# Transposing X unscaled and bringing the norm's factor in as a row, in a two-block fp32 kernel on one Trainium2 core

## The chip, the cores and the metric

The kernel runs on one core of a Trainium2 chip. The metric is the device time of one execution in microseconds (us). TensorE is called PE below, its weight loads PEld, VectorE is DVE, ScalarE is ACT, GpSimd is POOL and SyncE is SP, as in the profile.

## The reference

X is 256 rows of 1024 numbers (fp32). Two blocks of a transformer run over it: first one mixer and its MLP, then a second block of two layers (a convolution and an attention, each with an MLP). Cut to what matters here:

```python
def rms_norm(x, g):
    return x * lax.rsqrt(jnp.mean(x * x, axis=-1, keepdims=True) + EPS) * g
# first block
h = rms_norm(x, g_mix_pre)
x = x + rms_norm(mixer(h) @ w_out, g_mix_post)
h = rms_norm(x, g_ff_pre)
x = x + rms_norm(jnp.square(jax.nn.relu(h @ w_ff_in)) @ w_ff_out, g_ff_post)
# second block, for each of two layers; sh, sc, g are modulation vectors of length 1024
h = rms_norm(x, mix_norm_g) * (1.0 + sc1) + sh1
x = x + g1 * (conv if layer == 0 else attention)(h)
h = rms_norm(x, mlp_norm_g) * (1.0 + sc2) + sh2
x = x + g2 * (jnp.square(jax.nn.relu(h @ w1)) @ w2)
```

So there are six norms of X. They are called norm 0 to norm 5 below: ahead of the mixer's input product (0), the first MLP (1), the convolution (2), the second MLP (3), the attention's QKV product (4) and the third MLP (5).

## The kernel before

**Products.** Every weight is streamed once from HBM in units of 128 x 2048 numbers (1 MB), through a ring of four slots. ACT writes a rounded copy `hi` of a unit (L345), DVE the remainder `lo` (L356), and PE takes three products for each pair of tiles: hi by hi, hi by lo, lo by hi (L407). The activation is split in the same way, into `hTh` and `hTl`, and it is needed transposed: 8 pieces (k = 0 to 7) of 128 channels by 256 rows of X. `unit_w` multiplies one unit of weights by 4 or 8 of the pieces and runs k in its innermost loop, `unit_x` the same with the activation as the stationary side. One unit of an MLP's first product is 48 matmuls of 256 columns.

**A norm, before.** The rows of X lie on the partitions, in two tiles tt = 0, 1. ACT squares three of the four quarters of X (tt by column half) and DVE the last one (`square_last`, L626). `rstd_fast` then makes the factor 1/sqrt(mean) of each row: a sum (L573), a first guess by ACT (Ln and Exp), three short steps on DVE (L578, L579, L581). DVE writes `diag_n` (L621), a diagonal matrix of the factors for each tile. PE fills the time with `stay_warm`, products nobody reads (L648), and then multiplies X by that diagonal (`transposes`, L444): this transposes a tile and scales its rows at once. ACT and DVE split the result into hTh and hTl: for norms 0 and 1 straight from PSUM (L457, L481), for norms 2 to 5 over a whole copy, made in turns by ACT and DVE (L463, L488; then L470, L494). The first product of the stage starts when four pieces of hTl are there:

```python
pe.wait_ge(hT_lo, 8 * (2, 5, 8)[m] + 4)
unit_w(pe, u0, None, hTh, hTl, 0, 4, True)
pe.wait_ge(hT_lo, 8 * (2, 5, 8)[m] + 8)
unit_w(pe, u0 + 1, None, hTh, hTl, 4, 4, False)
```

**Behind the norm of an MLP.** DVE goes on in program order with `late_steps`: half a chunk of the modulation vectors (`ada_unit`: L888 and three of L891, on 128 x 512), a `lo` split, the other half chunk (four of L891), another `lo` split. PE, behind the first two units, sums that chunk over the partitions (`ada_sum`, L868, four columns), and for that it waits until all eight steps are done:

```python
pe.wait_ge(ada_step, number * 8 + 16)
```

At the same time ACT takes the ReLU of the two units (L786) and POOL squares it (L820).

**Order of the work.** Each engine has its program written out by hand and runs it in order; semaphores join them. Norms 1 and 2 follow `post_dve`, in which the branch itself is normalised: DVE multiplies PSUM by a gain row (L691), takes the factor of tile 0 by `rsqrt` (13 short instructions, L521 to L532) and of tile 1 by `rstd_fast`, and adds each to X in one instruction of 1024 columns (L698). Norms 3 to 5 follow `gated_dve`, which updates X in quarters (L707, L708).

## Time and profile before

| | |
|---|---|
| median of 3 runs | 1093.14 us (1093.11 to 1094.69) |
| profiled execution, its own time | 1095.8 us |
| its span, first to last instruction | 1094.0 us |
| mean granted TensorE clock | 0.989 of full speed |
| busy: PE, DVE, ACT, POOL | 96%, 64%, 45%, 10% of the span |
| read from HBM | 215 MB |

A share of busy time is an average over the whole span. PE counts as busy in the `stay_warm` products too, so its 96% hides that nothing useful runs there at the start of a stage.

### The profile page before, as it was taken

Reading aid. Unit: us, or ns where it says so; the run is one execution under the profiler, and the core shown is the slowest. Engines: PE = TensorE matmul, PEld = TensorE weight load, DVE = VectorE, ACT = ScalarE, POOL = GpSimd, SP = SyncE. Lnnn points to the kernel's source line nnn. Section 1 sums busy time; section 2 is a strip of 40 time slices with the busy share of each in tenths; the row PEclk is TensorE's granted clock in tenths of the full one; section 3 lists DMA queues with packets and bytes.
Section 4 is the critical chain, followed back from the end, with each engine's and each line's share of the span. In section 5 each row is a group of like instructions: output and inputs, shape, how many; then the busy total and the mean of one; then the engine's idle time right before and its main releaser. Section 6 shows DMA issues by size and latency. Waiting matters only on the chain.

```text
span 1094.0 us, 16799 instructions
## 1 busy us (share of the span) xinstructions
PE 1049.3 (96%) x6872; PEld 924.3 (84%) x6872; DVE 701.1 (64%) x823; ACT 491.8 (45%) x553; POOL 111.4 (10%) x76
## 2 busy tenths in 40 slices
PE   6999998999999999998899999999998799999998
PEld 6997776799999998985789999998886579999996
...
GB/s 281 314 291 159 128 116 160 287 79 315 288 254 288 272 281 106 220 257 197 86 74 341 264 288 259 288 266 134 193 192 123 109 78 155 192 185 198 185 161 39
DMA packets 118716, 221.58 MB, mean 203 GB/s; under 512 B 6338, under 2 KB 20740, under 8 KB 118660
## 3 DMA queue, kind: packets, MB, share of 16 engines
...
q14 instruction: 16, 0.13, 0.0%
...
## 4 chain that ended last, share of the span: by engine, by line
PE 82%; DVE 7%; ACT 4%; issue 3%; DMA 2%; SPq 1%; ACTq 0%; DVEq 0%
PE ps L407 77%; ACT hi L345 2%; PE ps L868 2%; DVE lo L356 1%; PE ps L444 1%; DVE ada_acc L891 1%; DMA ada_raw<-in_ada_w 1%; PE ps L722 1%; PE ps L648 1%; DVE stat L1915 1%; DMA raw<-in_w_in 0%; DVE hTl L494 0%; PE ps L1192 0%; ACT aS L1626 0%; DVE aS L1910 0%
## 5 line engine op out<-in xcount | busy, mean ns | idle before, releaser
L356 DVE TENSOR_TENSOR lo<-raw,hi 128x2048 fp32r<-128x2048 f32 x153 | 356.1, 2334 | 274.8 <-ACT hi L345 274.0
L345 ACT ACTIVATE hi<-raw 128x2048 fp32r<-128x2048 f32 x153 | 292.2, 1913 | 331.1 <-PE ps L407 314.0
L407 PE MATMUL ps<-hTh,hi 128*128 128x256 f32 x992 | 282.7, 285 | 2.0 <-DVE hTl L494 1.9
L407 PE MATMUL ps<-hTh,lo 128*128 128x256 f32 x992 | 280.7, 283 | 0.0
L407 PE MATMUL ps<-hTl,hi 128*128 128x256 f32 x992 | 280.7, 283 | 0.0
L407 PEld LDWEIGHTS ps<-hTh,hi 128*128 128x128 f32 x992 | 190.3, 192 | 3.8 <-DVE hTl L494 2.5
L407 PEld LDWEIGHTS ps<-hTl,hi 128*128 128x128 f32 x992 | 190.3, 192 | 0.3
L407 PEld LDWEIGHTS ps<-hTh,lo 128*128 128x128 f32 x992 | 190.3, 192 | 0.0
L407 PE MATMUL ps<-hi,hidh 128*128 128x512 f32 x416 | 163.0, 392 | 0.4 <-DVEq L643 0.4
L407 PE MATMUL ps<-hi,hidl 128*128 128x512 f32 x416 | 162.1, 390 | 0.0
L407 PE MATMUL ps<-lo,hidh 128*128 128x512 f32 x416 | 162.1, 390 | 0.0
L407 PE MATMUL ps<-hi,hTh 128*128 128x512 f32 (+1 forms) x320 | 127.8, 399 | 3.6 <-DVE hTl L1021 2.9
L891 DVE SCALAR_TENSOR_TENSOR ada_acc<-ada_raw,cond,ada_acc 128x512 f32<-128x512 f32 x161 | 125.7, 781 | 7.6 <-DMA ada_raw<-in_ada_w 2.7
L407 PE MATMUL ps<-hi,hTl 128*128 128x512 f32 (+1 forms) x320 | 124.9, 390 | 0.0
L407 PE MATMUL ps<-lo,hTh 128*128 128x512 f32 (+1 forms) x320 | 124.7, 390 | 0.0
L820 POOL TENSOR_TENSOR sqr<-relu 128x1024 f32<-128x1024 f32 x24 | 50.1, 2090 | 566.1 <-ACT relu L786 566.1
L407 PEld LDWEIGHTS ps<-lo,hidh 128*128 128x128 f32 x416 | 78.1, 188 | 16.6
L407 PEld LDWEIGHTS ps<-hi,hidh 128*128 128x128 f32 x416 | 78.2, 188 | 16.2 <-DVEq L643 0.8
L407 PEld LDWEIGHTS ps<-hi,hidl 128*128 128x128 f32 x416 | 78.2, 188 | 15.1
L407 PEld LDWEIGHTS ps<-hi,hTh 128*128 128x128 f32 x320 | 61.4, 192 | 18.6 <-issue 5.0
L407 PEld LDWEIGHTS ps<-lo,hTh 128*128 128x128 f32 x320 | 61.2, 191 | 12.8
L407 PEld LDWEIGHTS ps<-hi,hTl 128*128 128x128 f32 x320 | 61.5, 192 | 11.4
...
## 6 DMA issues: line engine op xcount, KB each, us to landing
...
```

The source lines that it names most:

```text
L345: nc.scalar.activation(hi[:, slot], raw[:, slot], ACT.Copy).then_inc(hi_made, 1)
L356: nc.vector.tensor_tensor(lo[:, slot], raw[:, slot], hi[:, slot].bitcast(F32), ALU.subtract).then_inc(lo_made, 1)
L407: return nc.tensor.matmul(o, lhs, rhs, start=start, stop=False, skip_group_check=True)
L444: last = nc.tensor.matmul(o, src(tt, k), diag[:, tt], start=True, stop=True)
L648: nc.tensor.matmul(ps[:, bank, 0:P], ones, ident, start=True, stop=True)
L722: last = nc.tensor.matmul(ps[:, 6 + k // 4, (k % 4) * P:(k % 4 + 1) * P], modT[:, m:m + 1].broadcast_to([P, P]), ident, start=True, stop=True)
L820: nc.gpsimd.tensor_tensor(sqr[:], relu[:], relu[:], ALU.mult).then_inc(sq_done, 1)
L868: last = nc.tensor.matmul(ps[:, bank, q:q + 1], acc[:, q * P:(q + 1) * P], ones[:, 0:1], start=True, stop=True)
L891: ins = nc.vector.scalar_tensor_tensor(out=acc[:], in0=w, scalar=s, in1=acc[:], op0=ALU.mult, op1=ALU.add)
L1915: ins = nc.vector.tensor_reduce(s_col(s, 2 * j, 2), aS[:, s % 4, :, c], AX.X, ALU.max)
```

## The change

Three things change together.

1. The diagonal is gone. PE transposes the quarters of X as they are, as soon as each is updated (`x_transposes`), and DVE and POOL do nothing for it. The factors of the rows come behind it as a row: PE multiplies the factor column, broadcast to 128 columns, by the identity (`row_of_rstd`), which leaves in PSUM a tile in which every partition holds the 256 factors. DVE scales all eight pieces by channel and by that row (`hT_dve`), ACT writes every hTh, and DVE every hTl.
2. The first units behind a norm run k by k (`unit_w_by_k`, `unit_x_by_k`): as soon as hTh[0] is there, all products with it; then those with hTl[0]; then k = 1, and so on. Behind norm 2 two units run side by side in this way, elsewhere one after the other.
3. `post_dve` finds the factor of tile 0 in the short way too, and updates X in quarters.

`stay_warm` runs 2 to 19 products at a norm instead of 14 to 36. The number of products with weights is the same.

```diff
+        def unit_w_by_k(pe, units, k0, banks, fill, nk=4):
...
+            for k in range(nk):
+                pe.wait_ge(hT_hi, 8 * fill + k0 + k + 1)
+                for u, bank in zip(units, banks):
+                    products(hi, hTh, k, u, bank, k0 == 0 and k == 0)
+                    products(lo, hTh, k, u, bank)
+                pe.wait_ge(hT_lo, 8 * fill + k0 + k + 1)
+                for u, bank in zip(units, banks):
+                    last = products(hi, hTl, k, u, bank)
+                    if k == nk - 1:
+                        last.then_inc(used, 1)
...
+        def x_transposes(pe, norm, ks, tt):
+
+            for k in ks:
+                o = tr_bank(k, NORM_BANKS[norm])[:, tt * P:(tt + 1) * P]
+                last = nc.tensor.transpose(o, X[:, tt, k * P:(k + 1) * P], ident)
...
+        def row_of_rstd(pe, norm):
+
+            pe.wait_ge(rstd_ok, norm + 1)
+            for tt in range(TT):
+                last = nc.tensor.matmul(ps[:, ROW_BANK[norm], tt * P:(tt + 1) * P],
+                                        rstd_col(0, tt).broadcast_to([P, P]), ident, start=True, stop=True)
+            last.then_inc(rstd_row, 1)
...
+        def hT_act(act, norm, bias=None):
+
+            for k in range(KT):
+                act.wait_ge(whole_made, 8 * norm + k + 1)
+                if bias is None:
+                    ins = nc.scalar.activation(hTh[:, k], whole[:, k], ACT.Copy)
+                else:
+                    ins = nc.scalar.activation(hTh[:, k], whole[:, k], ACT.Identity, bias=bias(k))
+                ins.then_inc(hT_hi, 1)
...
+        def hT_dve(dve, norm, b, scale, bias=None):
+
+            bank = ps[:, ROW_BANK[norm], 0:SEQ]
+            dve.wait_ge(rstd_row, norm + 1)
+            nc.vector.tensor_tensor(whole[:, 0], whole[:, 0], bank, ALU.mult).then_inc(whole_made, 1)
+            link(dve, nc.vector.tensor_copy(row_s[:], bank))
+            for kk in range(KT):
+                k = kk + 1
+                if k < KT:
+                    nc.vector.scalar_tensor_tensor(out=whole[:, k], in0=tr_bank(k, NORM_BANKS[norm]),
+                                                   scalar=scale(k), in1=row_s[:], op0=ALU.mult,
+                                                   op1=ALU.mult).then_inc(whole_made, 1)
+                dve.wait_ge(whole_made, 8 * norm + kk + 1)
+                dve.wait_ge(hT_hi, 8 * b + kk + 1)
...
             dve.wait_ge(ss_act, 3 * norm + 3)
-            rstd_fast(dve, NORM_ROOT[norm], 0, 0, TT)
-            diagonals_dve(dve)
+            mean_dve(dve, 0, 0, TT)
+            if norm:
+                first_scaled(dve, norm, scale)
+            newton_dve(dve, NORM_ROOT[norm], 0, 0, TT)
+            dve_inc(rstd_ok)
...
-        def norm_pe(pe, norm):
-            if norm == 4:
-                pe.wait_ge(row_kept, 2)
-            stay_warm((16, 34, 36, 14, 14, 14)[norm], bank=0 if norm == 5 else 7)
-            transposes(pe, lambda tt, k: X[:, tt, k * P:(k + 1) * P],
-                       [(diag_ok, norm + 1)] * 2, diag_n)
+        def norm_pe(pe, norm, between=None):
...
+            elif norm <= 2:
+                stay_warm(6, bank=5)
+                for tt in range(TT):
+                    if tt:
+                        stay_warm(4, bank=5 if norm == 1 else 2)
+                    pe.wait_ge(x_half, 2 * (norm - 1) + tt + 1)
+                    x_transposes(pe, norm, early, tt)
+                    pe.wait_ge(x_ver, 2 * (norm - 1) + tt + 1)
+                    x_transposes(pe, norm, late, tt)
+                stay_warm(4, bank=5 if norm == 1 else 2)
+            else:
+                if norm == 4:
+                    pe.wait_ge(row_kept, 2)
+                for ks, done in ((early, x_half), (late, x_ver)):
+                    for tt in range(TT):
+                        pe.wait_ge(done, 2 * (norm - 1) + tt + 1)
+                        x_transposes(pe, norm, ks, tt)
+            row_of_rstd(pe, norm)
+            stay_warm(5 if norm else 2, bank=WARM_BANK[norm])
...
+            for q, (tt, c) in enumerate(QUARTERS[:3]):
+                dve.wait_ge(ss_post, 4 * which + q + 1)
+                link(dve, times_row(tt, c))
+            mean_dve(dve, 1, 0, 1)
+            newton_dve(dve, POST_ROOT[which], 1, 0, 1)
+            update(0, 0, x_half)
+            dve.wait_ge(ss_post, 4 * which + 4)
+            mean_dve(dve, 1, 1, 1)
+            update(0, 1, x_ver)
+            link(dve, times_row(1, 1))
+            newton_dve(dve, POST_ROOT[which] + 1, 1, 1, 1)
+            update(1, 0, x_half)
+            update(1, 1, x_ver)
```

`first_scaled` multiplies piece 0 by its channel factor from PSUM, ahead of the three short steps, so that only the row is missing from it. For norm 0 the transposes run at the start, the first `hi` and `lo` split stay ahead of the pieces, and the later parameter transposes (L1158, L1160) move from between the first two units to behind them.

The rows that follow are instructions in program order, with what each waits for. On PE, this is the beginning of the second MLP before: the warming products, the scaled transposes, and the first products, whose first waits for four pieces of hTl.

```order
L648 MATMUL ps<-cst 128x128 x14
L444 MATMUL ps<-diag_n,X 128x128 [waits diag_ok]
L444 MATMUL ps<-diag_n,X 128x128 x7
L444 MATMUL ps<-diag_n,X 128x128 [waits diag_ok]
L444 MATMUL ps<-diag_n,X 128x128 x7
L407 MATMUL ps<-hTh,hi 128x256 [waits lo_made,hT_lo]
L407 MATMUL ps<-hTl,hi 128x256
```

The same place on PE in the changed kernel (`stat` holds the factors; L493 is `x_transposes`, L501 `row_of_rstd`, L445 a product with a weight):

```order
L493 MATMUL ps<-cst,X 128x128 [waits x_ver]
L493 MATMUL ps<-cst,X 128x128 x3
L501 MATMUL ps<-cst,stat 128x128 [waits rstd_ok]
L501 MATMUL ps<-cst,stat 128x128
L707 MATMUL ps<-cst 128x128 x5
L445 MATMUL ps<-hTh,hi 128x256 [waits hT_hi,lo_made]
L445 MATMUL ps<-hTh,hi 128x256 x3
L445 MATMUL ps<-hTh,lo 128x256 x4
L445 MATMUL ps<-hTl,hi 128x256 [waits hT_lo]
```

The wait for the factors moved from the first of the transposes to the one small product behind them, and the first product with a weight waits for one piece of hTh instead of four of hTl.

On DVE, norm 3 before, from the factor's last step to the `lo` split behind the modulation chunk:

```order
L581 SCALAR_TENSOR_TENSOR stat<-stat 128x2 [waits dve_chain]
L621 TENSOR_TENSOR diag_n<-cst,stat 128x256 [waits dve_chain]
L488 TENSOR_SCALAR whole<-ps,modT 128x256 [waits tr_done]
L488 TENSOR_SCALAR whole<-ps,modT 128x256
L494 TENSOR_TENSOR hTl<-whole,hTh 128x256 [waits hT_hi] x2
L494 TENSOR_TENSOR hTl<-whole,hTh 128x256 [waits whole_dve,hT_hi] x2
L488 TENSOR_SCALAR whole<-ps,modT 128x256 [waits tr_done]
L488 TENSOR_SCALAR whole<-ps,modT 128x256
L494 TENSOR_TENSOR hTl<-whole,hTh 128x256 [waits hT_hi] x2
L494 TENSOR_TENSOR hTl<-whole,hTh 128x256 [waits whole_dve,hT_hi] x2
L888 TENSOR_SCALAR ada_acc<-ada_raw,cond 128x512 [waits ada_landed0]
```

and in the changed kernel, where the pair of L545 and L554 stands seven times and L981 is what L891 was:

```order
L533 TENSOR_SCALAR whole<-ps,modT 128x256 [waits tr_done]
L637 TENSOR_TENSOR stat<-stat 128x2 [waits guess_ok,mean_ok,dve_chain]
L638 SCALAR_TENSOR_TENSOR stat<-stat 128x2 [waits dve_chain]
L640 SCALAR_TENSOR_TENSOR stat<-stat 128x2 [waits dve_chain]
L540 TENSOR_TENSOR whole<-whole,ps 128x256 [waits dve_chain,rstd_row]
L541 COPY row_s<-ps 128x256
L545 SCALAR_TENSOR_TENSOR whole<-ps,modT,row_s 128x256 [waits dve_chain]
L554 SCALAR_TENSOR_TENSOR hTl<-whole,modT,hTh 128x256 [waits hT_hi,whole_made]
...
L978 TENSOR_SCALAR ada_acc<-ada_raw,cond 128x512 [waits ada_landed0]
L981 SCALAR_TENSOR_TENSOR ada_acc<-ada_raw,cond,ada_acc 128x512 [waits ada_step] x3
```

DVE now makes all eight whole copies instead of four; what follows (the modulation chunk, the `lo` splits) is in the order of before.

## Rows read from the trace of the kernel before

**Rows 1.** The page: the chain that ended last, by engine.
```profile
PE 82%; DVE 7%; ACT 4%; issue 3%; DMA 2%; SPq 1%; ACTq 0%; DVEq 0%
```

**Rows 2.** Timeline of PE at norm 2: start, duration, engine, line, operation, [idle before, releaser].
```profile
429.46 3.84 PE L444 MATMUL ps<-diag_n,X 128*128 128x128 f32 x32 [1.03 <-DVE diag_n L621]
433.94 0.39 PE L407 MATMUL ps<-hTh,hi 128*128 128x256 f32 x1 [0.64 <-DVE hTl L494]
```

**Rows 3.** Timeline of DVE at norm 2, in and behind `post_dve`.
```profile
419.89 0.16 DVE L521 SCALAR_TENSOR_TENSOR stat<-stat 128x1 f32<-128x1 f32 x1
...
422.27 1.28 DVE L698 SCALAR_TENSOR_TENSOR X<-y_tmp,stat,X 128x1024 f32<-128x1024 f32 x1
...
424.93 0.16 DVE L578 TENSOR_TENSOR stat<-stat 128x1 f32<-128x1 f32 x1 [0.57 <-ACT stat L568]
...
425.51 1.28 DVE L698 SCALAR_TENSOR_TENSOR X<-sqr,stat,X 128x1024 f32<-128x1024 f32 x1
...
428.98 0.42 DVE L621 TENSOR_TENSOR diag_n<-cst,stat 128x256 f32<-128x256 f32 x1
```

**Rows 4.** Timeline rows of operations like the new ones, several places.
```profile
17.84 3.49 DVE L481 SCALAR_TENSOR_TENSOR hTl<-ps,pcol,hTh 128x256 fp32r<-128x256 f32 x8 [3.34 <-ACT hTh L457]
...
561.83 1.02 ACT L463 ACTIVATE whole<-ps,modT 128x256 f32<-128x256 f32 x2 [0.57 <-PE ps L444]
```

**Rows 5.** Timeline of DVE at norm 3, four pieces of hTl.
```profile
563.64 1.42 DVE L494 TENSOR_TENSOR hTl<-whole,hTh 128x256 fp32r<-128x256 f32 x4
```

**Rows 6.** Timeline of DVE and PE at norm 4.
```profile
758.84 0.42 DVE L621 TENSOR_TENSOR diag_n<-cst,stat 128x256 f32<-128x256 f32 x1
...
763.80 0.50 PE L407 MATMUL ps<-hi,hTh 128*128 128x512 f32 x1 [0.64 <-DVE hTl L494]
```

**Rows 7.** Chain in order of time at the start of the first MLP.
```profile
232.03 11.78 PE ps L407 x96
```

**Rows 8.** Timeline of DVE, PE and POOL, norm 1 and behind it.
```profile
227.66 0.43 DVE L621 TENSOR_TENSOR diag_n<-cst,stat 128x256 f32<-128x256 f32 x1
...
233.68 0.48 DVE L888 TENSOR_SCALAR ada_acc<-ada_raw,cond 128x512 f32<-128x512 f32 x1
...
238.64 3.11 DVE L891 SCALAR_TENSOR_TENSOR ada_acc<-ada_raw,cond,ada_acc 128x512 f32<-128x512 f32 x4
...
244.01 1.03 PE L868 MATMUL ps<-cst,ada_acc 128*128 128x1 f32 x8
...
244.96 2.94 POOL L820 TENSOR_TENSOR sqr<-relu 128x1024 f32<-128x1024 f32 x1 [53.25 <-ACT relu L786]
```

**Rows 9.** Timeline of DVE and PE at norm 3, PE behind norm 5.
```profile
560.15 0.43 DVE L621 TENSOR_TENSOR diag_n<-cst,stat 128x256 f32<-128x256 f32 x1
...
577.10 1.03 PE L868 MATMUL ps<-cst,ada_acc 128*128 128x1 f32 x8
...
917.65 1.03 PE L868 MATMUL ps<-cst,ada_acc 128*128 128x1 f32 x8
```

**Rows 10.** Timeline of DVE and POOL in the convolution.
```profile
478.40 3.07 DVE L891 SCALAR_TENSOR_TENSOR ada_acc<-ada_raw,cond,ada_acc 128x512 f32<-128x512 f32 x2
...
478.47 2.45 POOL L1982 TENSOR_TENSOR dw_sel<-cst,pcol 128x1024 f32<-128x1024 f32 x1 [1.18 <-PE ps L407]
```

**Rows 11.** Windows: stretch, its length, busy time of PE, PEld, DVE, ACT, POOL, granted clock, DMA.
```profile
193.50:199.50 6.00, 5.98 (x18) 5.08 (x19) 5.33 (x10) 1.32 (x4) 0.00 (x0) 0.50 0.51 139
...
529.70:532.50 2.80, 0.00 (x0) 0.03 (x1) 2.58 (x8) 1.99 (x5) 0.00 (x0) 1.00 0.00 0
534.20:537.40 3.20, 3.20 (x9) 2.23 (x8) 2.91 (x8) 2.73 (x7) 0.00 (x0) 0.50 0.00 0
...
823.90:827.50 3.60, 3.60 (x14) 2.96 (x15) 1.29 (x1) 1.84 (x3) 0.00 (x0) 0.55 0.92 294
828.00:832.00 4.00, 4.00 (x19) 3.25 (x18) 0.00 (x0) 0.00 (x0) 0.00 (x0) 1.00 0.59 217
```

**Rows 12.** Timeline of ACT at the start of the kernel.
```profile
20.31 5.51 ACT L345 ACTIVATE hi<-raw 128x2048 fp32r<-128x2048 f32 x3
```

More of the change, by code:

```diff
@@ L582, in rstd_fast, with norm_act @@
                                                      op1=ALU.mult))
[L584 to L586 removed]
+        NORM_ROOT, POST_ROOT = (0, 3, 6, 7, 8, 9), (1, 4)
+        def norm_act(act, norm, free, bias=None):
             def square_x(tt, c):
@@ L613, in norm_act @@
                 act_step(act, free - 1)
-            if before is not None:
-                before()
-            hT_act(act, fill, b, scale, bias, mod)
-        def diagonals_dve(dve):
-            i2, y2 = ident.unsqueeze(1).broadcast_to([P, TT, P]), rstd_col(0, 0, TT).unsqueeze(2)
-            nc.vector.tensor_tensor(diag_n[:], i2, y2.broadcast_to([P, TT, P]), ALU.mult).then_inc(diag_ok, 1)
+            else:
+                split_hi(act, 0, 0)
+            hT_act(act, norm, bias)
         def square_last(dve):
@@ L1296, in conv_in @@
                     pe.wait_ge(u_ok, 2 * (c - 1))
+                units = [U_CIN + 2 * c + h for h in range(2)]
+                if c == 0:
+                    unit_w_by_k(pe, units, 0, [chunk_bank(c), chunk_bank(c) + 1], 3, nk=8)
+                    return
                 for h in range(2):
-                    unit_w(pe, U_CIN + 2 * c + h, None, hTh, hTl, 0, chunk_bank(c) + h, True, nk=8,
-                           half=(hT_lo, 32) if c == h == 0 else None)
+                    unit_w(pe, units[h], None, hTh, hTl, 0, chunk_bank(c) + h, True, nk=8)
             def conv(c):
```

266 lines of the change are left out of this document (133 added, 133 removed).

## The prediction

> **What bounds the kernel now.** I read the chain on the profile's page first: 82% of it lies on PE, and no other engine has more than 7% [rows 1]. So what counts is where PE stands still or does nothing useful, and whatever lets its first useful product start earlier moves the rest of the program, if PE then isn't stopped by the next thing. The timeline at norm 2 shows such a place: DVE begins `diag_n` at 428.98 [rows 3], PE transposes from 429.46 for 3.84 us, stops 0.64 us for the fourth hTl, and its first weight product stands at 433.94 [rows 2]. From "the factor is ready" (called D, the start of `diag_n`) to that product (called S) 4.96 us pass. At norms 3 to 5 it is the same: 758.84 to 763.80 at norm 4 [rows 6]. At norm 1 it is 4.37 (227.66 to 232.03) [rows 7, 8]. Next I looked at what PE waits for behind the first two units. At norms 1, 3 and 5 it is the modulation sum at L868 (244.01, 577.10, 917.65) [rows 8, 9]; behind norms 2 and 4 it is no such sum. So an earlier S has two different fates.
>
> **The new start, step by step.** At D the row can be made. It is two fp32 products; such products (the 32 of the transposes are 16 in two passes) run at 3.84/32 = 0.12 us a pass [rows 2], a last one lasts 0.28. Four passes, the last full, and 0.17 for the two hand-overs give T = D + 0.8, the row's arrival at DVE. This last figure is an estimate.
>
> From T: DVE multiplies piece 0 by the row. A DVE operation of 256 columns with PSUM as a source takes 3.49/8 = 0.44 [rows 4], diag_n, of the same size without, 0.43 [rows 3]: 0.42 at the pitch of a run. ACT then copies: a pass of 256 columns with a bias from PSUM takes 1.02/2 = 0.51 [rows 4]; without a bias I take 0.41 (both estimates for SBUF). With 0.1 for the hand-over PE starts at T + 0.93 without a bias (norm 1) and at T + 1.0 with one, so at D + 1.73 and D + 1.8.
>
> At norms 3, 4 and 5 D doesn't move: `first_scaled` lies under the wait for ACT's guess, which norm 2 shows as a stall of half a microsecond on DVE ahead of L578 [rows 3]. There S gains 4.96 − 1.8 = 3.2 us (4: 3.15).
>
> At norms 1 and 2 D moves too. Tile 0's 13 steps run from 419.89 to 422.27, 2.38 us; three short ones take 425.51 − 424.93 = 0.58 [rows 3], and the mean that now stands apart is one step more, 0.19. That leaves 1.6 saved (the guess is hidden by `times_row`); X in quarters costs nothing, as two of 512 columns follow each other without a stall. So D is 427.4 at norm 2 and S 427.4 + 1.8 = 429.2: 4.75 us earlier. At norm 1 I take 1.5: D = 226.2, S = 227.95, 4.1 us earlier.
>
> **Does DVE keep pace?** A piece now costs DVE a product with the row (0.42 between 3.11/8 = 0.39 for 256 of an SBUF operation [rows 8] and 0.44) and an hTl: 1.42/4 = 0.355 [rows 5] without a bias, 0.40 with one, as it becomes a three-operand step. That is 0.76 or 0.82 for a k, where PE needs 11.78/8 = 1.47 for a k's 12 products of one unit [rows 7]. So PE sets the pace with 0.65 us to spare per k, and the fine interleaving costs it nothing. The row copy adds 0.4 once. DVE ends its pieces at T + 0.84 + 7 x 0.42 + 8 x 0.34 = T + 6.4, and T + 6.9 with a bias.
>
> **What comes behind: norms 2 and 4.** Behind norm 4 the QKV units run on, and the attention follows PE: 3.15 kept. Behind norm 2 two units run side by side and release both banks only at the end; the copies and DVE work of the convolution follow PE's last result, so I count 4.75 whole.
>
> **Norms 1, 3, 5: the modulation sum.** PE reaches it at S + 11.98 (244.01 − 232.03) [rows 7, 8] = T + 12.9 at norm 1 and T + 13.0 at norms 3, 5. DVE starts the chunk when its pieces are done. From L888 (233.68) to the second half's four L891 (238.64) 4.96 us pass; three of those four take 3 x 0.78 = 2.35, so the fourth starts 7.3 us after L888 [rows 8]: T + 13.7 at norm 1, T + 14.2 at 3 and 5, and is over 0.75 later. So PE waits here in any case: the start of PE gained more than DVE's end.
>
> And there is POOL. It asks for the square of the ReLU at S + 12.93 (244.96 − 232.03) [rows 8], T + 13.86 or T + 13.93. POOL and DVE don't run two-SBUF-source operations at once in this trace: while POOL's 2.45 us product stands at 478.47, two L891 of DVE from 478.40 take 3.07, where two take 1.55 elsewhere [rows 8, 10]. One that has begun goes through, the next waits until POOL is done. At norm 1 the fourth L891 has begun (13.7 < 13.86): the sum starts at T + 14.45 = 241.5, 2.5 before. At norms 3 and 5 POOL comes 0.3 before it: the step waits to T + 16.5 = 577.5, 0.4 later than before.
>
> There PE stands from T + 13.0 to T + 16.5, 3.5 us. Such a stop isn't free. PE did nothing from 529.70 to 532.50, and from 534.20 to 537.40 the granted clock is 0.50, the 1.2 GHz level [rows 11]. Half pace for about 3.4 us costs 1.7. So norms 3 and 5 give −0.4 − 1.7 = −2.1 each.
>
> **Norm 0.** ACT makes all eight hTh, so `hi` of the second unit starts behind them instead of at 20.31 [rows 12]; the transposes at the start run behind the same DMA. The pieces gain, the second unit loses; −0.2, with 0.5 either way.
>
> **The sum.** −0.2 + 2.5 + 4.75 − 2.1 + 3.15 − 2.1 = 6.0 us. It is made in an execution of 1095.8 us (span 1094.0), so 1089.8 there. The median of the three runs is 1093.14, 2.66 less; the forecast for it is 1087.1.
>
> **The rivals.** Unless told otherwise the other terms stay.
>
> *A, the forecast*, 0.38. Its own range, 1085.4 to 1088.8, is from the estimates of T and S (0.2 at each of five norms) and of the clock (0.3 twice).
>
> *B, POOL doesn't get in front.* If DVE's pieces end 0.3 us sooner, or ACT's ReLU is later, the fourth step goes first at norms 3 and 5. The sum starts at T + 14.95 = 576.0, 1.1 earlier, the stop is 2 us, and I charge no clock. Both are 3.2 better: total 12.4, 1080.7. For it: the margin is 0.3 us out of sums of eight estimated pieces. Against: the bias makes each hTl dearer, and nothing in it is rounded against A. 0.25.
>
> *C, POOL first at norm 1 too.* The margin is 0.16 there. The sum starts at 243.0, 1.0 earlier, the clock costs 1.7: −0.7 instead of +2.5. Total 2.8, 1090.3. 0.18.
>
> *E, the convolution gives part back.* Two units release their banks together at the end instead of one after the other, so that whoever copies the first unit's result starts later than before by nearly a unit less the gain. If this copy and the DMAs behind it end last there, half of norm 2's gain stays (2.3): total 3.5, 1089.6. Against it: behind norm 2 DVE and ACT are far from full when the units run. 0.07.
>
> *D, the clock doesn't rise in the new norm.* Before, 14 to 36 warming products and 32 transposing passes fill PE ahead of S; now it is mostly short raw transposes. If those don't hold the clock, the row's passes and the warm products (14 in all) run at 0.24 instead of 0.12, PE comes free at D + 3.4, and then works at the 1.2 GHz level for 3.4 us or so: a start at that level lasted 6.0 us at 193.50 (granted 0.50) [rows 11]. Norm 2 would give 1.45 instead of 4.75, norm 1 0.65, norm 4 −0.15, norms 3 and 5 −0.1, norm 0 −0.2: total 1.55, 1091.6. The trace speaks against it: from 823.90 to 827.50 eight transposes lie in PE's work, at a granted clock of 0.55, and from 828.00 it is 1.00 [rows 11]: they did not keep it down. 0.08. The Trainium skill ("TensorE: Matmul & The Clock Gate", Part 4) has this rule: a transpose in PE's transpose mode doesn't count as PE being busy, and the full clock doesn't engage for it. By the stretch at 823.90 this trace doesn't agree; the rule's own case, transposes and nothing else, no stretch here shows.
>
> *F, slower: DVE falls behind k by k.* A piece is now a round trip: DVE's product, ACT's hTh, DVE's hTl, and three hand-overs. If waiting inside it costs DVE x us per k more, the chunk behind is late by 8x at norms 1, 3 and 5, 24x in all, and the two-unit stages lose the rest of their slack. From 0.65 us of spare per k on, PE itself waits; at x = 0.25 the 6.0 us are gone by the chunks alone, from x = 0.34 the kernel is slower by over 0.2% (6.0 − 24 x 0.34 = −2.2), at x = 0.5 the total is −6.0: 1099.1. Against it: before, the same pieces ran two and two without a wait on ACT (four hTl in 1.42) [rows 5], and a product is ahead of each hTl as cover. 0.04.
>
> **How the numbers follow.** 0.2%, 2.2 us, is about what a measurement of this kernel can tell from no change: below 1090.95 is faster, above 1095.33 slower. A, B, most of C, E and a little of D are faster: 0.83. The rest of C and D is within: 0.13. F: 0.04. B stands at 1080.7 and D at 1091.6; with 0.9 beyond B and 0.2 beyond D the range is 1079.8 to 1091.8, which leaves F and the tails out.
>
> **What would show it.** In the changed kernel's own time, less what was gained before: the first L445 comes 1.7 to 1.8 us behind DVE's last factor step at every norm (right: A to C); no stop of PE between k's (F has them); DVE's last hTl ends 6.4 to 6.9 us behind the row. At the sums of norms 1, 3 and 5, L891's successor with a length near 2.3 instead of 0.75 means that POOL went first; a granted clock of 0.5 behind it is the charge of 1.7. A granted clock of 0.5 from the first L445 on is D. A long wait of the convolution's first copy is E. The prediction is most at risk at the chunks: 0.3 us there decide over 3.2 us, twice.

## The result, and the profile after

| | before | changed |
|---|---|---|
| median of 13 runs each | 1094.69 us (1093.11 to 1095.79) | 1089.59 us (1082.32 to 1091.84) |
| changed to before | | 0.9948, 95% interval 0.993 to 0.9966 |
| the profiled execution, its own time | 1095.8 us | 1087.14 us |
| its span | 1094.0 us | 1085.4 us |
| mean granted TensorE clock in it | 0.989 | 0.980 |

By the ratio the change gains 5.7 us (0.52%, 3.7 to 7.7 us by its interval), between the medians 5.1; 6.0 were forecast. Two things stand out before any row is read. The changed kernel's runs lie 9.5 us apart, those of before 2.7; and its profiled execution, 2.5 us below its median, gained 8.7 us, while its mean clock fell. So one trace doesn't tell the whole of this kernel.

The chain by engine, of the changed kernel, against [rows 1]: PE is still what bounds it, with DVE three points up.

```profile
PE 81%; DVE 10%; ACT 4%; issue 3%; DMA 1%; SPq 0%; DVEq 0%; ACTq 0%
```

**The new start.** The timeline of DVE and PE at norm 2 after, against [rows 2, 3]:

```profile
425.82 0.16 DVE L640 SCALAR_TENSOR_TENSOR stat<-stat 128x2 f32<-128x2 f32 x1
426.09 0.71 PE L501 MATMUL ps<-cst,stat 128*128 128x128 f32 x4 [0.59 <-DVEq L702]
...
426.84 0.42 DVE L540 TENSOR_TENSOR whole<-whole,ps 128x256 f32<-128x256 f32 x1 [0.86 <-PE ps L501]
...
427.95 0.47 PE L445 MATMUL ps<-hTh,hi 128*128 128x256 f32 x2
```

The factor's last step stands at 425.82, the row reaches DVE 0.82 us after the factor is ready (426.02, the next slot of DVE behind that step), and PE's first weight product comes 1.93 us after it. Between the k's PE shows no idle time. The same at norm 4, against [rows 6]:

```profile
753.01 0.16 DVE L640 SCALAR_TENSOR_TENSOR stat<-stat 128x2 f32<-128x2 f32 x1
...
755.14 0.47 PE L445 MATMUL ps<-hi,hTh 128*128 128x512 f32 x1
```

At norm 1 it is 1.85 us (225.61 to 227.46), at norm 5 1.94 (890.08 to 892.02). Norm 3 is different (timeline of DVE and PE after):

```profile
553.51 0.16 DVE L640 SCALAR_TENSOR_TENSOR stat<-stat 128x2 f32<-128x2 f32 x1
553.79 1.03 PE L501 MATMUL ps<-cst,stat 128*128 128x128 f32 x4 [1.49 <-DVEq L702]
556.61 0.97 PE L445 MATMUL ps<-hTh,hi 128*128 128x256 f32 x3
```

PE stood (waited and did nothing) 1.49 us ahead of the row, works at half clock from 554.0 on, and its first weight product comes 2.9 us behind the factor. DVE's last hTl ends 6.6 us behind the row's arrival at norm 1, 7.5 at norm 2 and 7.1 at norms 3 to 5; 6.4 and 6.9 were forecast.

**The sums behind norms 1, 3 and 5.** DVE, POOL and PE, timeline after, against [rows 8, 9]; norm 1 first, then norm 3, then norm 5:

```profile
240.29 0.75 DVE L981 SCALAR_TENSOR_TENSOR ada_acc<-ada_raw,cond,ada_acc 128x512 f32<-128x512 f32 x1
240.34 2.45 POOL L910 TENSOR_TENSOR sqr<-relu 128x1024 f32<-128x1024 f32 x1 [49.15 <-ACT relu L876]
241.09 1.05 PE L958 MATMUL ps<-cst,ada_acc 128*128 128x1 f32 x8 [1.56 <-DVE ada_acc L981]
...
566.87 3.11 DVE L981 SCALAR_TENSOR_TENSOR ada_acc<-ada_raw,cond,ada_acc 128x512 f32<-128x512 f32 x4
569.86 1.89 POOL L910 TENSOR_TENSOR sqr<-relu 128x1024 f32<-128x1024 f32 x1 [53.61 <-ACT relu L876]
...
902.92 4.62 DVE L981 SCALAR_TENSOR_TENSOR ada_acc<-ada_raw,cond,ada_acc 128x512 f32<-128x512 f32 x4
904.90 2.09 POOL L910 TENSOR_TENSOR sqr<-relu 128x1024 f32<-128x1024 f32 x1 [44.22 <-ACT relu L876]
907.59 0.60 PE L958 MATMUL ps<-cst,ada_acc 128*128 128x1 f32 x4 [3.50 <-DVE ada_acc L981]
```

At norm 1 DVE's last step starts 0.05 us ahead of POOL's square and runs its 0.75. At norm 5 POOL comes first, the four steps take 4.62 instead of 3.1, and PE stands 3.50 us. At norm 3 DVE's last step (569.23) was 0.6 ahead of POOL, and PE stood 0.97 us (sum at 570.04). The last step stands 14.37 us behind the row's arrival (554.86 and 890.90) at norms 3 and 5 alike; POOL's square stands 14.00 behind it at norm 5 and 15.00 at norm 3, where PE had started a microsecond late. So what put DVE first at norm 3 is the half clock at its start; e7 below bears that out. Then the clock, by stretches of the changed kernel (stretch, its length, busy time of PE, PEld, DVE, ACT, POOL, granted clock, DMA):

```profile
14.70:21.40 6.70, 5.55 (x26) 5.58 (x27) 6.41 (x18) 3.81 (x9) 0.00 (x0) 0.50 1.07 369
243.40:246.80 3.40, 3.40 (x18) 3.40 (x17) 3.40 (x2) 0.49 (x1) 0.00 (x0) 0.50 0.77 264
554.00:557.30 3.30, 3.30 (x17) 3.30 (x17) 2.40 (x7) 2.15 (x4) 0.00 (x0) 0.50 0.00 0
571.20:574.40 3.20, 3.20 (x16) 3.20 (x16) 3.20 (x2) 1.44 (x2) 0.56 (x1) 0.50 1.02 390
909.20:912.30 3.10, 3.10 (x17) 3.10 (x17) 3.10 (x3) 0.00 (x0) 0.00 (x0) 0.50 0.35 73
```

Half clock, the 1.2 GHz level, behind all three sums, and at the starts of norms 0 and 3. Before, none of these places had it. The longest of these stretches, at norm 0, comes with a stand of PE of 3.65 us (from 12.20); no run here fills that one.

**Where the 8.7 us of this execution come from.** The same split of ACT (L345, by its number in the program, counted from 0) is taken in both traces at places between the norms:

| place | before | after | shift | gained since the place above |
|---|---|---|---|---|
| ahead of norm 1 (split 31) | 215.27 | 214.76 | −0.51 | 0.5 (norm 0) |
| in the first MLP (40) | 281.07 | 279.54 | −1.53 | 1.0 (norm 1) |
| in the convolution (68) | 459.77 | 453.75 | −6.02 | 4.5 (norm 2) |
| ahead of norm 3 (76) | 559.37 | 552.90 | −6.47 | 0.45 |
| in the second MLP (84) | 614.15 | 608.48 | −5.67 | −0.8 (norm 3) |
| in the QKV products (112) | 787.75 | 779.01 | −8.74 | 3.1 (norm 4) |
| ahead of norm 5 (124) | 899.73 | 889.26 | −10.47 | 1.7 (attention) |
| in the third MLP (130) | 941.36 | 932.70 | −8.67 | −1.8 (norm 5) |

The change doesn't touch the attention. There before has a stretch of half clock at 824.3 that after hasn't (812 to 832: 1.00); 1.5 of its 1.7 us are that. PE stands 2.62 us in both kernels at this place (from 821.23 before and from 812.49 after): behind the one stand the clock falls, behind the other it doesn't.

### The profile page after: what moved, and what is told of

Read it like the earlier page. It is cut to its first block, busy times and chain, and to the rows that moved or that the text cites. A ratio compares the mean times of both kernels' runs of the same rounds, so it can differ in the third digit from the quotient of the medians.

```text
span 1085.4 us, 16414 instructions
## 1 busy us (share of the span) xinstructions
PE 1032.0 (95%) x6654; PEld 906.7 (84%) x6654; DVE 711.7 (66%) x847; ACT 490.3 (45%) x541; POOL 108.5 (10%) x76
## 4 chain that ended last, share of the span: by engine, by line
PE 81%; DVE 10%; ACT 4%; issue 3%; DMA 1%; SPq 0%; DVEq 0%; ACTq 0%
PE ps L445 77%; ACT hi L345 2%; DVE ada_acc L981 2%; PE ps L958 2%; DVE lo L356 1%; DMA raw<-in_w_in 1%; DMA ada_raw<-in_ada_w 1%; PE ps L814 1%; DVE hTl L554 1%; DVE whole L545 1%; DVE stat L2007 1%; DVE X L777 1%; DVE hTl L551 0%; PE ps L1285 0%; ACT aS L1718 0%
## 5 line engine op out<-in xcount | busy, mean ns | idle before, releaser
L345 ACT ACTIVATE hi<-raw 128x2048 fp32r<-128x2048 f32 x153 | 292.2, 1912 | 328.6 <-PE ps L445 309.3
L445 PE MATMUL ps<-hTh,hi 128*128 128x256 f32 x992 | 268.0, 289 | 4.5 <-ACT hTh L525 3.7
L445 PE MATMUL ps<-hTh,lo 128*128 128x256 f32 x992 | 265.3, 286 | 0.0
L445 PE MATMUL ps<-hTl,hi 128*128 128x256 f32 x992 | 264.0, 286 | 0.0
L445 PEld LDWEIGHTS ps<-hTh,hi 128*128 128x128 f32 x992 | 185.8, 196 | 6.0 <-issue 4.6
L445 PEld LDWEIGHTS ps<-hTh,lo 128*128 128x128 f32 x992 | 185.2, 195 | 0.0
L445 PEld LDWEIGHTS ps<-hTl,hi 128*128 128x128 f32 x992 | 184.8, 195 | 0.3
L445 PE MATMUL ps<-hi,hidh 128*128 128x512 f32 x416 | 163.0, 392 | 0.4 <-DVEq L702 0.4
L445 PE MATMUL ps<-hi,hidl 128*128 128x512 f32 x416 | 162.1, 390 | 0.0
L445 PE MATMUL ps<-lo,hidh 128*128 128x512 f32 x416 | 162.0, 390 | 0.0
L981 DVE SCALAR_TENSOR_TENSOR ada_acc<-ada_raw,cond,ada_acc 128x512 f32<-128x512 f32 x161 | 127.2, 790 | 7.2 <-DMA ada_raw<-in_ada_w 2.3
L445 PE MATMUL ps<-hi,hTh 128*128 128x512 f32 (+1 forms) x320 | 126.9, 397 | 2.9 <-DVE hTl L1111 2.9
L445 PE MATMUL ps<-lo,hTh 128*128 128x512 f32 (+1 forms) x320 | 124.3, 388 | 0.0
L445 PE MATMUL ps<-hi,hTl 128*128 128x512 f32 (+1 forms) x320 | 123.3, 389 | 0.0
L910 POOL TENSOR_TENSOR sqr<-relu 128x1024 f32<-128x1024 f32 x24 | 46.8, 1950 | 570.5 <-ACT relu L876 570.5
L445 PEld LDWEIGHTS ps<-lo,hidh 128*128 128x128 f32 x416 | 78.1, 188 | 16.6
L445 PEld LDWEIGHTS ps<-hi,hidh 128*128 128x128 f32 x416 | 78.2, 188 | 16.1 <-DVEq L702 0.8
L445 PEld LDWEIGHTS ps<-hi,hidl 128*128 128x128 f32 x416 | 78.2, 188 | 15.3
L445 PEld LDWEIGHTS ps<-hi,hTh 128*128 128x128 f32 x320 | 61.1, 191 | 17.1 <-issue 5.1
L445 PEld LDWEIGHTS ps<-lo,hTh 128*128 128x128 f32 x320 | 61.0, 191 | 12.6
L445 PEld LDWEIGHTS ps<-hi,hTl 128*128 128x128 f32 x320 | 61.1, 191 | 11.4
```

The source lines that it names most:

```text
L345: nc.scalar.activation(hi[:, slot], raw[:, slot], ACT.Copy).then_inc(hi_made, 1)
L445: return nc.tensor.matmul(o, lhs, rhs, start=start, stop=False, skip_group_check=True)
L910: nc.gpsimd.tensor_tensor(sqr[:], relu[:], relu[:], ALU.mult).then_inc(sq_done, 1)
L981: ins = nc.vector.scalar_tensor_tensor(out=acc[:], in0=w, scalar=s, in1=acc[:], op0=ALU.mult, op1=ALU.add)
```

## The experiments

The kernel before, measured beside each, had 1094.4 to 1094.9 us. "Changed" is the changed kernel, 1089.59.

| run | median (lowest to highest), us | ratio to before, 95% |
|---|---|---|
| changed | 1089.59 (1082.32 to 1091.84) | 0.9948 (0.993 to 0.9966) |
| e1: sums' wait filled, too long | 1088.73 (1087.09 to 1093.24) | 0.9956 (0.9941 to 0.997) |
| e1b: filled to its length | 1085.15 (1082.79 to 1090.54) | 0.9931 (0.9909 to 0.9953) |
| e2: chunk first | 1082.13 (1079.81 to 1082.38) | 0.9877 (0.9862 to 0.9891) |
| e3: long root | 1092.67 (1087.69 to 1095.63) | 0.9982 (0.997 to 0.9994) |
| e4: no unit k by k | 1100.28 (1098.57 to 1102.46) | 1.0051 (1.0039 to 1.0063) |
| e5: k by k alone, in before | 1092.61 (1090.9 to 1094.73) | 0.9984 (0.9975 to 0.9992) |
| e6: warmed by transposes, in before | 1094.0 (1092.95 to 1095.74) | 0.9996 (0.9987 to 1.0005) |
| e7: filled ahead of the row | 1092.28 (1090.31 to 1095.09) | 0.9977 (0.9965 to 0.9988) |
| e8: e2 and e7 together | 1082.73 (1081.54 to 1082.96) | 0.989 (0.9876 to 0.9904) |
| e9: MLPs tile by tile | 1089.77 (1088.96 to 1090.86) | 0.9955 (0.9942 to 0.9968) |
| e10: DVE always before POOL | 1087.1 (1082.59 to 1088.72) | 0.9923 (0.9906 to 0.994) |
| e11: POOL always before DVE | 1098.74 (1093.25 to 1100.14) | 1.0031 (1.0018 to 1.0045) |

**e1, the wait at the sums filled.**

```diff
+            stay_warm((14, 10, 28)[m], bank=7)
             ada_sum(pe, ADA_HEAD[m][0])
```

> The changed kernel, and in it PE fills its wait for the modulation sum at norms 1, 3 and 5 with 14, 10 and 28 products nobody reads (1.6, 1.2 and 3.3 us at 0.12 us a pass). My theory (the start of PE gains 3 to 5 us at each norm, but at norms 1, 3 and 5 PE then stands at the sum, and behind the stand the granted clock falls to 0.5 for 3.4 us, which costs 1.7): the sums start where they do in the changed kernel, the clock stays at 1.00 behind them, and the kernel takes up to 3 x 1.7 = 5.1 us less than the changed one: about 1085, with less spread between executions. Rival 1 (the clock falls because the start of a norm holds only short transposes): no difference, 1089.6, and a granted clock of 0.5 behind the sums as before.

The time missed, by a slip of mine that the trace shows: a product of `stay_warm` is two passes. PE and DVE at norm 1, timeline:

```profile
239.53 3.37 PE L707 MATMUL ps<-cst 128*128 128x128 f32 x28
...
241.09 3.98 DVE L356 TENSOR_TENSOR lo<-raw,hi 128x2048 fp32r<-128x2048 f32 x1
242.74 0.95 PE L959 MATMUL ps<-cst,ada_acc 128*128 128x1 f32 x8
```

The window behind it:

```profile
243.60:247.00 3.40, 3.40 (x30) 3.40 (x31) 3.40 (x2) 0.42 (x1) 0.00 (x0) 1.00 0.77 248
```

The chunk was whole by 241.09, when DVE goes on to its next split, but PE was at its fill until 242.9: the sum came 1.65 us late. The clock stayed at 1.00, behind the other two sums as well.

**e1b, half as many** (6, 4, 14).

> As the run with the sums' wait filled, but with 6, 4 and 14 products: there each product was two passes, so that the fill lasted 3.4 and 6.5 us and the sums of norms 1 and 5 came 1.6 and 2.5 us late, while the clock stayed at 1.00. Filled to the length of the wait (1.4, 1.0 and 3.4 us), my theory gives the sums their time of the changed kernel and no fall of the clock behind them: 1084 to 1086. If it stays at 1089, what the clock costs there is given back elsewhere.

PE and POOL at norm 1, timeline:

```profile
238.27 1.58 PE L707 MATMUL ps<-cst 128*128 128x128 f32 x12
239.21 2.44 POOL L911 TENSOR_TENSOR sqr<-relu 128x1024 f32<-128x1024 f32 x1 [47.63 <-ACT relu L877]
239.96 1.05 PE L959 MATMUL ps<-cst,ada_acc 128*128 128x1 f32 x8
```

Windows behind norms 1 and 5:

```profile
242.00:245.40 3.40, 3.40 (x31) 3.40 (x30) 3.40 (x2) 0.76 (x1) 0.00 (x0) 1.00 0.82 289
906.00:909.40 3.40, 3.40 (x30) 3.40 (x30) 3.40 (x3) 0.00 (x0) 0.00 (x0) 1.00 0.36 80
```

DVE, POOL and PE at norm 1 go as my theory had it: the sum starts 0.75 us behind POOL's square, as in the changed kernel, and the clock stays at 1.00 behind all three sums. The stretches of the two traces between the same splits as in the table above show what that is worth: 1.5 us less at each of the norms 1, 3 and 5 (63.29 instead of 64.78, 54.12 instead of 55.58, 41.95 instead of 43.44). That the stand is what lets the clock fall there is shown by these, and by e1. The median is 4.4 us lower, as expected, but that alone proves little: the runs still lie 7.8 us apart, and the intervals of the two kernels overlap. At norm 4 this trace has a fall that the changed kernel's hasn't (from 749.1), and loses 1.4 us by it.

**e2, the chunk ahead of the splits.**

```diff
             for h in range(2):
                 if chunk is not None:
                     ada_unit(dve, chunk[0], h, skipped)
+            for h in range(2):
                 dve_step(dve, last - 1 + h)
```

> The changed kernel, and behind norms 1, 3 and 5 DVE does both halves of the modulation chunk first and both lo splits after them. My theory: the chunk is whole 2.3 us earlier, at about the time at which PE arrives and before POOL asks for its square, so that nothing but the ReLU and the lo split of the next unit (ends about 2 us behind PE's arrival) is waited for: 0.8 us less stand at norms 1 and 3, 3 us less at norm 5, and fewer falls of the clock: 1080 to 1084. Rival 2 (what costs there is the exclusion between POOL's square and DVE alone): only norm 5 gains, 1.5 us and one fall of the clock: 1087. Rival 1: 1087 too, with the falls still there.

DVE and PE at norm 1, timeline:

```profile
235.72 4.76 DVE L981 SCALAR_TENSOR_TENSOR ada_acc<-ada_raw,cond,ada_acc 128x512 f32<-128x512 f32 x6
240.39 6.19 DVE L356 TENSOR_TENSOR lo<-raw,hi 128x2048 fp32r<-128x2048 f32 x2
240.83 1.03 PE L958 MATMUL ps<-cst,ada_acc 128*128 128x1 f32 x8
242.73 0.39 PE L445 MATMUL ps<-hTh,hi 128*128 128x256 f32 x1 [0.87 <-DVE lo L356]
```

The window behind it:

```profile
243.00:246.40 3.40, 3.40 (x30) 3.40 (x30) 3.40 (x1) 1.56 (x2) 1.43 (x1) 1.00 0.60 188
```

PE no longer waits for the sum, only 0.87 us for the split behind it; the clock stays at 1.00 behind all three sums. 12.7 us faster than before and 7.5 faster than the changed kernel, inside what was expected; the runs lie 2.6 us apart. The clock still falls at the starts of norms 3 and 5 (from 555.2 and 889.7). This version beats both kernels. The swap was tried on top of the change alone, not in the kernel before.

**e9, the MLPs' first units tile by tile.**

```diff
-            for h in range(2):
-                unit_w_by_k(pe, [u0 + h], 4 * h, [4], (2, 5, 8)[m])
+            pe.wait_ge(hT_lo, 8 * (2, 5, 8)[m] + 4)
+            unit_w(pe, u0, None, hTh, hTl, 0, 4, True)
+            pe.wait_ge(hT_lo, 8 * (2, 5, 8)[m] + 8)
+            unit_w(pe, u0 + 1, None, hTh, hTl, 4, 4, False)
```

> The changed kernel, but at norms 1, 3 and 5 the first two units run tile by tile again and wait for four pieces of hTl; norms 0, 2 and 4 stay k by k. My theory: PE starts there 3.1 us later, arrives at the sum when it is (nearly) ready, doesn't stand, and the clock doesn't fall: the sums start where they do in the changed kernel (norm 5 perhaps as well, since POOL's square moves back by 3 us too, behind DVE's chunk: 1.5 earlier), so that the earlier start is shown to be worth nothing there; 1085 to 1088. Rival 3 (the start k by k is what gains at these norms too): 3 x 2 to 3 us slower, 1096 or more.

PE at norm 1, timeline:

```profile
230.15 0.39 PE L445 MATMUL ps<-hTh,hi 128*128 128x256 f32 x1 [2.76 <-DVE hTl L551]
```

PE starts 2.7 us later at norm 1, and the median is that of the changed kernel (0.2 us apart), a little above my range. So at the MLPs the earlier start gains nothing in the changed kernel. Two things are mixed in that. PE's idle time of 3 us moved ahead of the first product, and in this trace the clock falls behind it at norms 3 and 5 (3.4 us each, from 560.4 and 898.3) instead of behind the sums, where PE doesn't stand any more. And POOL's square comes 2.9 to 4.1 us behind DVE's last step, so that DVE is always first. Against e10 below, in which DVE is always first and the units run k by k, e9 is 2.7 us slower, and each of its runs is slower than each of e10's: the earlier start is worth something once POOL can't come in front. The runs of e9 lie within 1.9 us.

**e4, no unit k by k.** Conv and QKV too wait for their pieces of hTl and run tile by tile (`unit_w`, `unit_x`, as before the change).

> The changed kernel with all first units tile by tile, each waiting for its four (eight) pieces of hTl as before the change; the row, the raw transposes and the short root stay. My theory: as with the MLPs alone, and norms 2 and 4 lose the 3.1 us between the first hTh and the fourth hTl each, so that of their gains of 4.5 and 3.1 only 1.4 and 0 are left: 1092 to 1094, about the time before the change. The row and the order k by k gain only together. Rival: the row alone brings most of the gain (the factor's wait gone from 32 passes to 4): 1090.

PE at norm 2, timeline:

```profile
431.06 0.48 PE L454 MATMUL ps<-hTh,hi 128*128 128x256 f32 x1 [3.00 <-DVE hTl L563]
```

Windows behind norms 2, 3 and 4:

```profile
431.20:434.50 3.30, 3.30 (x16) 3.30 (x17) 2.67 (x8) 2.50 (x4) 0.00 (x0) 0.50 0.00 0
560.90:571.00 10.10, 7.91 (x37) 7.61 (x37) 9.71 (x22) 4.24 (x9) 0.00 (x0) 0.50 0.00 1
762.30:769.00 6.70, 4.50 (x15) 3.65 (x15) 6.41 (x17) 4.23 (x9) 0.00 (x0) 0.50 0.00 0
```

5.4 us slower than before, 6 above my range. The 3 us between row and fourth hTl were as expected; what I left out is that PE has nothing to do in them, where before the 32 passes filled that time. The clock falls for the 3.3, 10 and 6.7 us of these windows, and behind norm 5 as well (3.4 us from 909.1). The row and the raw transposes without the order k by k are a loss in this form; with PE kept at work in the 3 us they might not be, which no run here tries.

**e5, the order k by k alone.** In the kernel before, the first units behind norms 2 and 4 run by `unit_w_by_k` and `unit_x_by_k`.

> The kernel before the change, with the first units behind norms 2 and 4 k by k (the other norms, the diagonal, the root as they were). My theory: the first hTh stands only behind the 32 scaled transposes, 0.4 to 1 us ahead of the fourth hTl, so that each of the two starts gains 0.5 to 1 us: 1093 to 1094. The order k by k is worth 3 us and more only with the row.

1092.61, 1.8 us faster, slightly more than expected. PE starts 4.07 us behind D at norm 2 (427.85 to 431.92) instead of 4.96. Together with e4: row and root without the order −5.4 (the falls of the clock included), the order alone +1.8, all together +5.1 in the medians.

**e3, the long root of tile 0.**

```diff
             mean_dve(dve, 1, 0, 1)
-            newton_dve(dve, POST_ROOT[which], 1, 0, 1)
+            dve.wait_ge(guess_ok, POST_ROOT[which] + 1)
+            rsqrt(dve, rstd_col(1, 0), ss_col(1, 0, 0), stat[:, 26:27], stat[:, 18:19], D, ss_col(1, 1, 0))
```

> The changed kernel with the 13 steps of before for the factor of tile 0 in post_dve; X is still updated in quarters. My theory: D comes 1.6 us later at norms 1 and 2, and at norm 1 DVE's chunk and the sum come 1.6 later too: 3 us slower than the changed kernel, 1092 to 1093. Rival: the short root hides nothing, since PE's last transposes or ACT's squares end last: 1090.

3.1 us slower than the changed kernel, as the 1.5 + 1.6 of the prediction, but that agreement is in part luck: its trace has POOL first at norm 1, and from split 31 to split 40 it takes 4.3 us longer than the changed kernel's, not 1.5. At norm 2, where no sum follows, it takes 1.5 us longer (split 40 to split 68, 175.69 instead of 174.21), and this is the clean reading of what the short root hides.

**e6, do transposes hold the clock?**

```diff
-            for _ in range(n):
-                nc.tensor.matmul(ps[:, bank, 0:P], ones, ident, start=True, stop=True)
+            for _ in range(2 * n):
+                nc.tensor.transpose(ps[:, bank, 0:P], ones, ident)
```

> The kernel before the change, in which each stay_warm product (two passes) is two transposes of the same tile (one pass each). If transposes hold the clock as products do, nothing changes: 1094.9, a granted clock of 1.00 at the starts of norms 1 to 5. If they don't (the rule of the Trainium skill, TensorE: Matmul & The Clock Gate, Part 4), PE counts as idle for 4 us and more at norms 1 and 2 and about 2 us at the others: falls to 0.5 at norms 1 and 2 at least, 1.7 us each or more, 1098 and up.

PE at norm 2, timeline (L648 are now transposes):

```profile
419.88 8.02 PE L648 MATMUL ps<-cst 128*128 128x128 f32 x72
```

The window around it:

```profile
421.00:434.00 13.00, 11.12 (x99) 10.69 (x98) 9.13 (x27) 8.22 (x21) 0.00 (x0) 1.00 0.00 1
```

No difference (0.9996), and no fall. 8 us of fp32 transposes of 128 x 128 and nothing else keep the granted clock at 1.00 here as products do. The Trainium skill (TensorE: Matmul & The Clock Gate, Part 4) states that transposes don't count as PE being busy; for these transposes the measurement says otherwise, and it decides. Rival D's mechanism is out. Its sign, half clock at the start of a norm, did appear at norm 3, behind the stand of 1.49 us ahead of the row; the next run and e8 fill that stand.

**e7, the wait ahead of the row filled.**

```diff
+            if norm > 2:
+                stay_warm((6, 6, 7)[norm - 3], bank=WARM_BANK[norm])
             row_of_rstd(pe, norm)
```

> The changed kernel, and at norms 3, 4 and 5 PE runs 6, 6 and 7 products nobody reads between the raw transposes and the row, where it stands 1.5, 1.5 and 1.8 us in the changed one. My theory: this stand is what lets the clock fall at the start of norm 3 (a granted clock of 0.5 from 553.9 in the profile), and in some executions at norms 4 and 5: the row comes at the same time and the fall is gone: 1 to 1.5 us faster in the median, 1088. If the sums alone make the clock fall: no difference.

2.7 us slower instead of 1 to 1.5 faster. Its trace (timeline of DVE, POOL and PE) shows one loss at norm 1, which the edit doesn't touch:

```profile
238.09 4.83 DVE L983 SCALAR_TENSOR_TENSOR ada_acc<-ada_raw,cond,ada_acc 128x512 f32<-128x512 f32 x4
240.49 1.89 POOL L912 TENSOR_TENSOR sqr<-relu 128x1024 f32<-128x1024 f32 x1 [49.07 <-ACT relu L878]
242.98 1.43 PE L960 MATMUL ps<-cst,ada_acc 128*128 128x1 f32 x8 [3.30 <-DVE ada_acc L983]
...
569.87 4.62 DVE L983 SCALAR_TENSOR_TENSOR ada_acc<-ada_raw,cond,ada_acc 128x512 f32<-128x512 f32 x4
571.85 2.09 POOL L912 TENSOR_TENSOR sqr<-relu 128x1024 f32<-128x1024 f32 x1 [52.40 <-ACT relu L878]
```

The window behind norm 1:

```profile
244.00:248.00 4.00, 4.00 (x19) 4.00 (x20) 4.00 (x3) 0.00 (x0) 0.00 (x0) 0.50 0.79 243
```

Here POOL was first at norm 1: DVE's four steps took 4.83 us, though the last of them asked first by a few hundredths. The programs of the changed kernel and of e7 are the same up to there, so, as far as one trace of each can tell, the order at norm 1 changes between executions. Over the five traces with this order of DVE's work that were taken so far (changed, e1, e1b, e3, e7) DVE's last step stands 0.04 to 0.06 us ahead of POOL's square at norm 1, and DVE won in three of them.

Norms 3 and 5 are no such tie. At norm 5 POOL is 0.37 us ahead in all five. At norm 3 DVE is 0.6 to 0.9 ahead in the four traces in which the clock falls at the start of the norm, and PE starts 2.6 to 2.9 us behind the factor; in e7, where the fill keeps the clock at 1.00 (551 to 558) and PE starts 1.93 behind it, POOL is 0.37 ahead as at norm 5. So the fill did what it was meant to, and thereby put POOL in front at norm 3: from split 76 to split 84 the trace of e7 takes 58.35 us, that of the changed kernel 55.58. The 2.8 us between them are this, and the 3.3 us at norm 1 (68.05 instead of 64.78) are the tie. That led to the next two.

**e10 and e11, the draw decided.** In e10 POOL waits for DVE's chunk, in e11 DVE's last step for POOL's square:

```diff
+            pool.wait_ge(ada_step, ADA_HEAD[m][0] * 8 + 16)
             square(8 * m, m > 0)
```

```diff
+                    if after is not None and h == 1 and k == 3:
+                        dve.wait_ge(*after)
```

Here `after` is `(sq_done, 8 * m + 1)`, for the chunks of `late_steps` alone.

> The changed kernel, and POOL's first square of each MLP waits until DVE's chunk of the modulation vectors is whole. The question is the spread of the changed kernel (1082.3 to 1091.8) and why norm 1 took 3 us more in the profiles of two variants that don't touch it. My theory now: at norms 1, 3 and 5 POOL's square and DVE's last step of the chunk start within 0.1 to 0.6 us of each other, and which comes first changes from execution to execution; POOL first costs 1.5 to 2 us of stand and another 1.7 by the clock. With DVE always first: sums 1.3 us at most behind DVE's steps, no long stand, 1082 to 1085 in the median, and a spread of 3 us or less. Rival 4 (the spread comes from where the clock falls elsewhere): median 1087 to 1089, spread as in the changed kernel.

> The changed kernel, and DVE's last step of the chunk behind norms 1, 3 and 5 waits until POOL's first square of that MLP is done. My theory: this is the bad end of the same draw at all three norms: PE stands 3 to 3.5 us at each sum, the clock falls behind each for 3.4 to 6.8 us, 1091 to 1094, and a small spread. If the order of the two is of no weight: 1089.6 plus a few tenths.

DVE, POOL and PE, timeline: of e10 at norm 5, then of e11 at norm 1:

```profile
906.04 3.11 DVE L982 SCALAR_TENSOR_TENSOR ada_acc<-ada_raw,cond,ada_acc 128x512 f32<-128x512 f32 x4
909.20 1.05 PE L959 MATMUL ps<-cst,ada_acc 128*128 128x1 f32 x8 [1.98 <-DVE ada_acc L982]
```

```profile
244.01 0.75 DVE L983 SCALAR_TENSOR_TENSOR ada_acc<-ada_raw,cond,ada_acc 128x512 f32<-128x512 f32 x1 [2.02 <-POOL sqr L910]
244.81 1.40 PE L958 MATMUL ps<-cst,ada_acc 128*128 128x1 f32 x7 [3.54 <-DVE ada_acc L983]
```

The windows behind them, e10 at norm 5 and e11 at norm 1:

```profile
911.00:917.00 6.00, 6.00 (x52) 6.00 (x51) 6.00 (x3) 1.83 (x2) 2.10 (x1) 1.00 0.69 186
...
245.20:251.80 6.60, 6.60 (x32) 6.60 (x33) 6.60 (x5) 0.00 (x0) 0.00 (x0) 0.50 0.84 283
```

The two orders lie 11.6 us apart, 3.9 for a norm. PE stands 1.55, 1.99 and 1.98 us at the three sums of e10 and 3.54, 4.05 and 3.53 us at those of e11. Behind them the clock is at half for 3.4, 3.4 and 0 us in e10 and for 6.8 us each in e11: at norm 5 of e10 a stand of 1.98 us has no fall behind it. The changed kernel stands between the two, and its interval overlaps that of e10. e11 is 5 us above my range, since I had not charged the second 3.4 us of half clock everywhere; e10 is 2 us above, and its runs still lie 6 us apart. So the order of the two can't be the only source of the spread.

**e8, e2 and e7 together.**

> The changed kernel with both halves of the chunk ahead of the lo splits (1082.1 alone) and PE kept at work between the raw transposes and the row at norms 3 to 5. My theory: with the chunk out of the draw with POOL, what the fill ahead of the row is worth can be seen: no fall of the clock at the starts of norms 3 and 5, which cost up to 1.7 us each in the run with the chunk first: 1079 to 1081. If the fill itself costs time (its own run had 1092.3, which I put down to POOL coming first at norm 1): 1084 or more.

The same stretch at the start of norm 3, first of e8, then of e2:

```profile
551.00:558.00 7.00, 6.63 (x53) 6.29 (x54) 5.75 (x18) 4.49 (x8) 0.00 (x0) 1.00 0.00 1
```

```profile
551.00:558.00 7.00, 5.31 (x33) 4.84 (x32) 5.72 (x16) 4.87 (x9) 0.00 (x0) 0.80 0.00 0
```

The fill does hold the clock there, and at norm 5 too (888 to 893: 1.00 in e8, 0.67 in e2), and yet the median is 0.6 us above e2's: expected were 1 to 3 below. The traces show why. PE starts earlier and runs into the next wait, DVE's `lo` split behind the chunk, which e2's PE meets when it is ready (timeline of PE in e8, behind the sums of norms 3 and 5):

```profile
569.46 0.38 PE L445 MATMUL ps<-hTh,hi 128*128 128x256 f32 x1 [1.15 <-DVE lo L356]
...
904.11 0.38 PE L445 MATMUL ps<-hTh,hi 128*128 128x256 f32 x1 [1.15 <-DVE lo L356]
```

From the factor's last step to this product it is 16.40 us in e8 (553.06 and 887.71) and 16.39 and 16.40 in e2 (554.27 to 570.66, 888.82 to 905.22): what PE gained at the start it stands at the split. Behind the second stand the clock falls in e8 (3.4 us from 905.7), which it doesn't in e2. So keeping the clock up ahead of a wait that doesn't move gains nothing. In e7 the fill had another price, POOL in front at norm 3, and the order of DVE's work in e8 takes that away.

## Why the prediction was right, and where it wasn't

**The start of a norm** came as worked out at four of the five. The first weight product stands 1.93 or 1.94 us behind the factor at norms 2, 4 and 5 and 1.85 at norm 1, forecast 1.8 and 1.73; at norm 3 it is 2.9. Gained at norm 2 4.5 (forecast 4.75), at norm 4 3.1 (3.15). e4 and e5 show that this is the row and the order k by k together, and e3 that 1.5 us of norm 2's gain hang on the root. PE didn't stop between the k's: rival F didn't happen. Nor did E: 4.5 us arrived in the convolution.

**The sums.** At norm 1 the sum stood at 241.09, and 0.5 us had been gained before it, so 241.6 in the time of the kernel before; forecast 241.5. At norm 5 case A came as told: POOL at T + 14.00 (forecast 13.93), DVE's last step at T + 14.37 (14.2), PE stood 3.50 us, and the norm cost 1.8, forecast 2.1. At norm 3 DVE was first (case B's branch) and the norm cost 0.8. One sum in the prediction doesn't add up: it takes an hTl at 0.34 us where its own row gives 0.355. With that DVE's pieces end at T + 6.6, which is what was measured (6.62), and the margin of 0.16 us by which DVE was to be first at norm 1 is gone; measured were 0.05.

**The step that failed** is in B: "the stop is 2 us, and I charge no clock". The same was left out at norm 1, where "the sum starts at T + 14.45 = 241.5, 2.5 before" was booked whole. Stands of 1.56 us at norm 1 and 0.97 at norm 3 were followed by 3.4 us of half clock too, so that norm 1 gave 1.0 instead of 2.5. e1b shows it: with PE at work until the sums come, each of the three norms takes 1.5 us less. The clock was left out at the start of norm 3 as well, where PE stands 1.49 us ahead of the row. That moved POOL's square from the T + 13.93 of the forecast to T + 15.00 and so put DVE first: B's order, for a reason that neither A nor B names.

**How near the number is, and how much of that is luck.** The 6.0 us were added up for the profiled execution, and there 8.7 came: norm 3 was taken 1.3 too low, the first norm 0.7 too low, norm 1 1.5 too high, the convolution gave 0.45 more, and the attention 1.7, which the change doesn't touch. Between the medians it was 5.1. The errors go both ways and offset in part; the forecast of 1087.1 also rests on the 1093.14 of three runs before, where thirteen have 1094.69. The profiled execution's 1087.14 is next to it by chance, and so is the median next to the 1089.6 of E, which didn't happen.

**The form of the argument** was off in one more way. A, B and C stood as rivals of which one would be true. By the traces they are outcomes of single executions. Which of POOL and DVE goes first at norm 1 changed between two programs that are the same up to there, and at norm 3 it hangs on whether the clock falls at the norm's start; e10 and e11 put 11.6 us between the two ends. The margins of 0.16 and 0.3 us were rightly named as the place where it is decided, and should have led to the forecast of a wide spread.

**Left open:** what else spreads the runs of e10 over 6 us, and when a stand of PE has a fall of the clock behind it and when it hasn't.
